# Squares of the norms summed over channel blocks on VectorE ahead of the ones-matmuls

## The reference

```python
D_MODEL = 1024
D_FF = 2816
EPS = 1e-6

def rmsnorm(x, g):
    xf = x.astype(jnp.float32)
    y = xf * lax.rsqrt(jnp.mean(xf * xf, axis=-1, keepdims=True) + EPS)
    return (y * g.astype(jnp.float32)).astype(x.dtype)

def swiglu(x, w_gate, w_up, w_down):
    return (jax.nn.silu(x @ w_gate) * (x @ w_up)) @ w_down

def trunk(h, pos, pool_prev, ret_prev, chunked):
    for i in range(DEPTH):
        xn = rmsnorm(h, norm_mix[i])
        if i % N_MIXERS == 0:
            mix, buf = multiscale_pool_mix(xn, ...)
        else:
            mix, s = retention_mix(xn, pos, ...)
        h = h + mix
        h = h + swiglu(rmsnorm(h, norm_ffn[i]), w_ffn_gate[i], w_ffn_up[i], w_ffn_down[i])
    return rmsnorm(h, norm_final), ...
```

## Time and profile before

| | |
|---|---|
| time, median of 3 runs | 1643.95 us (1643.01, 1643.95, 1694.63) |
| span of the profiled execution, slowest core (core 4) | 1656.3 us |
| spans of its 8 cores | 1629.7 to 1656.3 us |
| medians of the two dies | 1634.0 and 1640.6 us |
| PE busy on core 4 | 1594.7 us (96%) |
| DVE, ACT, POOL busy on core 4 | 735.8 (44%), 669.6 (40%), 355.5 us (21%) |
| mean granted TensorE clock, over the cores | 0.978 to 0.990 |

### The profile page before, as it was taken

One profiled execution on the slowest core, in us unless ns is written; L12 is line 12 of the kernel. 1 busy time (PEld: TensorE's weight loads), 2 busy tenths in 40 slices (PEclk: granted clock), 3 DMA queues, 4 the chain that ended last, 5 costly groups with the idle time before them and its releaser, 6 DMA issues.

```text
span 1656.3 us, 28455 instructions; the slowest of 8 cores (1629.7 to 1656.3 us)
## 1 busy us (share of the span) xinstructions
PE 1594.7 (96%) x9951; PEld 919.8 (56%) x10044; DVE 735.8 (44%) x1415; ACT 669.6 (40%) x1223; POOL 355.5 (21%) x584
## 2 busy tenths in 40 slices
PE   5999999999999989989999999999998899999997
PEld 3666666655555655444454444456554456666665
DVE  4432222634637362444363543356564556323225
ACT  4311022256465733545645424444664464110222
POOL 5110100334435221110101010013524146101000
PEclk8899999999999999999999999999999899999998
DMA  9157975787666778878989997876537531313432
GB/s 236 28 102 161 190 150 113 139 143 139 141 131 119 140 172 277 271 218 206 249 210 273 259 278 258 239 200 138 109 82 77 76 65 51 104 60 97 71 53 104
DMA packets 87449, 253.78 MB, mean 153 GB/s; under 512 B 17584, under 2 KB 24048, under 8 KB 87296
## 3 DMA queue, kind: packets, MB, share of 16 engines
q0 software_dynamic: 32656, 114.57, 37.2%
q1 hardware_dynamic: 54656, 137.40, 27.6%
HBM read 254.81 MB, written 73.27 MB: 198 GB/s over the span
## 4 chain that ended last, share of the span: by engine, by line
PE 89%; DMA 5%; DVE 2%; issue 2%; ACT 1%; POOL 1%; SPq 0%; DVEq 0%; POOLq 0%; ACTq 0%
PE pm L483 75%; PE psU L483 7%; PE psS L483 5%; DMA U<-U 2%; PE pm L491 1%; DMA cs_sb<-sret 1%; DMA cs_sb<-xtok 1%; DMA fb<-sret 1%; PE pm L487 0%; DMA fb<-xtok 0%; ACT on L500 0%; SPq L202 0%; DVE stt L982 0%; DVE hB L507 0%; DVE fb L516 0%
## 5 line engine op out<-in xcount | busy, mean ns | idle before, releaser
L483 PE MATMUL pm<-xn,w 128*128 128x512 bf16 (+8 forms) x4395 | 790.3, 337 | 3.7 <-DVE xn L516 1.1
L483 PEld LDWEIGHTS pm<-xn,w 128*128 128x128 bf16 x4432 | 433.5, 99 | 329.8 <-issue 20.8
L483 PE MATMUL pm<-U,w 128*128 128x512 bf16 (+6 forms) x2295 | 404.2, 333 | 4.0 <-DVE U L507 2.6
L483 PEld LDWEIGHTS pm<-U,w 128*128 128x128 bf16 x2310 | 224.2, 98 | 165.9 <-issue 21.7
L507 DVE TENSOR_TENSOR U<-pm,rot 128x512 bf16<-128x512 f32 (+5 forms) x206 | 121.2, 588 | 372.1 <-PE pm L483 344.0
L500 ACT ACTIVATE rot<-pm 128x512 bf16<-128x512 f32 (+6 forms) x190 | 98.3, 518 | 368.9 <-PE pm L483 364.5
L507 DVE TENSOR_TENSOR hB<-pm,hB 128x347 f32<-128x347 f32 (+4 forms) x143 | 76.2, 544 | 101.9 <-PE pm L483 101.1
L483 PE MATMUL pm<-w,xn 128*128 128x512 bf16 (+1 forms) x444 | 105.1, 381 | 1.1 <-DVE U L507 0.3
L507 POOL TENSOR_TENSOR U<-rot 128x352 bf16<-128x352 f32 (+2 forms) x96 | 93.1, 990 | 56.9 <-DVE rot L507 56.8
L507 DVE TENSOR_TENSOR hA<-pm,hA 128x512 f32<-128x512 f32 (+4 forms) x117 | 67.8, 588 | 83.3 <-PE pm L483 82.9
L507 DVE TENSOR_TENSOR rot<-pm,cs_sb 128x352 f32<-128x352 f32 (+2 forms) x170 | 79.3, 512 | 26.5 <-POOL U L507 14.8
(11 more groups left out here) (252 smaller groups left out, 1536.4 us busy)
## 6 DMA issues: line engine op xcount, KB each, us to landing
w<-c_gu POOLq DMA_DIRECT2D x49, 512.0 KB, 7.5
w<-w_gu POOLq DMA_DIRECT2D x39, 512.0 KB, 8.9
fb<-sret SPq DMA_DIRECT2D x38, 512.0 KB, 9.1
nrs<-fb SPq DMA_DIRECT2D x38, 512.0 KB, 9.3
w<-w_d POOLq DMA_DIRECT2D x32, 352.0 KB, 5.6
w<-c_d POOLq DMA_DIRECT2D x32, 352.0 KB, 6.1
c_gu<-w SPq DMA_DIRECT2D x17, 512.0 KB, 8.1
w<-w_qk POOLq DMA_DIRECT2D x16, 512.0 KB, 10.8
```

The lines of the kernel that those rows point to most:

```text
L483: return P.op('pe', lambda h: h.matmul(out, lhsT=lhsT, rhs=rhs, start=start, stop=stop, skip_group_check=skip), ins=[lhsT, rhs], outs=[out ...
```

## The change

`presum` adds squares of channel blocks to one another on DVE, in place and in bf16, as soon as `hadd` and the square of block m are recorded: at m = 2 block 1 += 0, at 3 block 2 += 1, at 4 block 3 += 2, at 6 block 5 += 4, at 7 block 6 += 5. Block 3 then holds the sum of blocks 0 to 3, block 6 that of 4 to 6, and block 7 is left as it is; `norm_stat` runs over blocks 3, 6 and 7. The norm after the pooling of `hA` keeps its eight. The sums over channels are rounded to bf16 at each addition.

```diff
--- before.py
+++ after.py
@@ -683,22 +683,30 @@
                     if e in handoff:
                         handoff.remove(e)
 
-        def norm_stat(r, sq, c0, n):
+        PRE = {2: (1, 0), 3: (2, 1), 4: (3, 2), 6: (5, 4), 7: (6, 5)}
+
+        def presum(sq, m, c0, n):
+
+            if m in PRE:
+                a, b = (sq[:, i, c0:c0 + n] for i in PRE[m])
+                tt(a, a, b, ALU.add)
+
+        def norm_stat(r, sq, c0, n, parts=(3, 6, 7)):
             pb = bank()
             tl = [(o, min(128, n - o)) for o in range(0, n, 128)]
             for i, (o, w) in enumerate(tl):
-                for c in range(8):
-                    mm(pb[0:w, i:i + 1], sq[:, c, c0 + o:c0 + o + w], onesb[:, 0:1], c == 0, c == 7)
+                for c in parts:
+                    mm(pb[0:w, i:i + 1], sq[:, c, c0 + o:c0 + o + w], onesb[:, 0:1], c == parts[0], c == parts[-1])
             return rsq(r[:, 0:len(tl)], pb[:, 0:len(tl)], 1024.0 * EPS, 128, len(tl))
 
-        def norm_gen(h, sq, wcol, c0, n, after=None, final=None, stat=None, pause=None):
+        def norm_gen(h, sq, wcol, c0, n, after=None, final=None, stat=None, pause=None, parts=(3, 6, 7)):
 
             yield after
             r = stat
             if r is None:
                 r = rs4[nrm['i'] % len(rs4)]
                 nrm['i'] += 1
-                yield norm_stat(r, sq, c0, n)
+                yield norm_stat(r, sq, c0, n, parts)
             if pause is not None:
                 yield 10 * pause
             tl = [(o, min(128, n - o)) for o in range(0, n, 128)]
@@ -830,7 +838,7 @@
                 late = [stat_a(i) for i in ahead[g:g + 1]]
                 if g < len(pumps):
                     wpump(pumps[g])
-            ng = norm_gen(hA, xn, C_NF0, c0, nt)
+            ng = norm_gen(hA, xn, C_NF0, c0, nt, parts=tuple(range(8)))
             yield next(ng)
             x = next(ng)
             for f in late:
@@ -939,6 +947,7 @@
                 hadd(h, m, c0, n, pb)
                 if last:
                     square(h, sq, m, c0, n)
+                    presum(sq, m, c0, n)
                 sd.poll()
             for fh in range(2):
                 j = 0
@@ -1219,6 +1228,7 @@
                 hadd(hh, m, c0, n, pb)
                 if exit_fn is not None:
                     sqlast[0] = tt(xn[:, m, c0:c0 + n], hh[:, m, c0:c0 + n], hh[:, m, c0:c0 + n], ALU.mult, "pool") if hf else square(hh, xn, m, c0, n)
+                    presum(xn, m, c0, n)
                 sd.poll()
             if exit_fn is not None:
                 for bi, (c0, n) in enumerate(blocks):
@@ -1460,6 +1470,7 @@
             for i, (c0, n) in enumerate(F512):
                 for m in range(8):
                     x = act(SQB[:, m, c0:c0 + n], hB[:, m, c0:c0 + n], ACT.Square)
+                    presum(SQB, m, c0, n)
                     yield 1.0
                 yield x
                 yield norm_stat(rsB[:, i, :], SQB, c0, n)
```

## The result

The changed kernel takes 1668.37 us (median of four runs, 1667.05 to 1675.89); the kernel before takes 1643.95 us (median of 1643.01, 1643.95 and 1646.16). Some runs of any of these kernels are slower, with a lower clock on the cores of a die (one run of before took 1694.63 us), and medians and ratios here are of the others. The ratio is 1.0148, 95% interval 1.012 to 1.0176: 1.5% slower, 24 us, where I had forecast 1638 us and a range of 1628 to 1649.

A forecast was written before the change was run, and what follows sets the result against it. PE was taken to bound the kernel, busy 1594.7 of 1656.3 us. From 1643.95 us, -9.1 for matmuls and +3.1 for the tail, additions hidden and reordering at nothing, gave 1638 us; range 1628 to 1649.

The forecast's parts named there:

- The removed matmuls: In the norm statistics on PE: 310 one-column matmuls fewer at 31 ns, 9.6 us, of which 9.1 us on the path.
- The first rival: DMA-heavy stages, 720 to 1130 us: saved matmuls only lengthen waits, losing up to 4.0 us; 1642 to 1647, chance 0.18.
- The added instructions: On DVE: 96 additions at 0.4 us, 38 us (20 to 54), hidden at nearly every stage end, priced at nothing.
- The third rival: Retention's last projection on `hB`: additions wait for POOL, up to 16 us, 1654; slower once over 6 reach PE; chance 0.09.
- The tail: Program's end, T being the last `hadd`'s end: six multiplies delay `rs_2`; last multiply from T + 7.7 to T + 10.8, 3.1 us longer.
- The second rival: Lower-clock stretches at 600 and 740 us, 3.4 us each: one gone 1635, both 1631, one more 1641; under 1633, chance 0.13.

The follow-up runs named there:

- mm_only: Kernel before in its old order, with three statistic matmuls for eight and no additions, so outputs change; 1637.48 us, ratio 0.9946 to before.
- adds_only: Kernel before in its old order, with all 96 additions and all eight matmuls kept, so outputs change; 1653.05 us, ratio 1.0044 to before.
- same_order: The whole change, with the planner's clocks kept so that the order is that of the kernel before; 1649.5 us, ratio 1.0034 to before.
- order_only: Instructions of the kernel before (eight matmuls, no additions) in the order the changed kernel's planner gives; 1665.94 us, ratio 1.0121 to before.
- exact_cost: The changed kernel with the planner told that a one-column matmul takes 0.031 us rather than 0.056; 1659.7 us, ratio 1.0095 to before.
- ffn_only: Old order; additions and three matmuls behind the FFNs and in the pooled half's statistic, but the old code behind the retentions; 1644.2 us, ratio 1.0014 to before.
- ffn_exits: Old order; additions and three matmuls only in norms behind the FFNs, not behind retentions or in the pooled half's statistic; 1645.68 us, ratio 1.001 to before.

## Why the prediction was wrong

**The removed matmuls: right.** 9.1 us were forecast; `mm_only` is 0.9946 of before, which is 8.9 us, and one costs 31 ns in both kernels. Where the Trainium skill, "TensorE: Matmul & The Clock Gate", section "Wait — 56ns, not 53.3ns?", has some 62 ns for matmuls that software decodes, the gain would be an estimated 19 us; the run excludes it. The first rival, the gain covered by transfers, is not borne out by the same run, whose gain is the whole 9 us; its interval, 5 to 13 us, leaves room for that rival's 4 us, and the stretches in question vary too much between cores to place them.

**The added instructions: the size too high, the cover too generous.** An addition at 341 to 347 columns takes 333 ns (0.40 forecast; DVE has 28 us more, 38 forecast). But they are not hidden everywhere: +7 us in `adds_only`, where the places behind the two retentions, in which DVE carries gates and statistics, take 3.2 and 3.3 us more, and PE waits 6.1 us a core for additions at the pooled half's statistic. I had looked at each stage end by itself and found room behind the last square, and had not asked what is queued around the addition in a retention and beside the state's products.

**The third rival: its mechanism is there, at a third of its price.** I gave additions that wait 1.1 us each for POOL up to 16 us. Measured are 4.8 us of waiting and additions stretched to 0.57 to 0.62 us, of which 3.3 us reach PE (88.5 to 91.8), about 1 of them POOL's doing. That stays below the rival's own turning point of 6. It is not what made the kernel slower. In the changed order 6.1 us are lost in that stretch, and on core 0 one wait of 4.4 us for a gate shows how; the chain is in DVE's timeline of after:

```profile
1388.56 0.81 DVE L507 TENSOR_TENSOR xn<-xn 128x347 bf16<-128x347 bf16 x1 [0.59 <-POOL xn L507]
1389.30 1.05 DVE L516 SCALAR_TENSOR_TENSOR xn<-hB,w,pm 128x347 bf16<-128x347 f32 x2
1390.27 0.51 DVE L507 TENSOR_TENSOR hB<-pm,hB 128x347 f32<-128x347 f32 x1
1390.70 0.32 DVE L507 TENSOR_TENSOR xn<-xn 128x347 bf16<-128x347 bf16 x1
1390.95 0.68 DVE L507 TENSOR_TENSOR U<-af,U 128x512 bf16<-128x512 f32 x1
```

```profile
1391.77 0.75 PE L483 MATMUL pm<-U,w 128*128 128x346 bf16 x4 [4.40 <-DVE U L507]
```

**The tail: right, and a little short.** Forecast was T + 10.8 for the last multiply's end and 3.1 us more. T is 1653.32 on core 4 of after, and the timeline has

```profile
1656.40 0.16 DVE L511 TENSOR_SCALAR rs<-pm 128x3 f32<-128x3 f32 x1
...
1658.61 4.95 DVE L516 SCALAR_TENSOR_TENSOR hB<-hB,w,pm 128x346 f32<-128x346 f32 x10 [1.08 <-PE pm L491]
```

`rs` at T + 3.1 (3.55 forecast) and the last multiply's end at 1663.56, T + 10.2, 2.5 us more than the T + 7.7 of before. The table's medians, which go on to the end of the last stores, give +3.7. `same_order` has 10.9: the tail's loss is all order.

**The step that failed** is this one: "In most places the rows are permuted by an instruction or two, and PE has other matmuls in between; I price that at nothing, with an uncertainty of some 4 us either way (a few waits of the size in the earlier trace rows, whose longest is 7.2 us)." I had even named a DMA transpose or state load issued later as what would make the prediction wrong, but bounded it by PE's waits and did not look through SyncE's list, where the transposes and their two neighbours stood in a new order. Costed by what the runs show: 10 us for the transposes, 4 for the two units of state, 2 for the norm's multiplies ahead of the first projection, 3 to 4.5 in the last part, 3 for the tail: 22 to 24 us, where `order_only` as a whole shows 20. The range's upper bound had room for half of the third rival (8 us) and some 3 us more, so it could not hold this. (Its closing sums are loose besides: twice the third rival is 1670 us, not 1677, and that rival's full price, 1654, lay outside the range.) The second step that failed is smaller: the additions were priced at nothing on the path, and cost 7. Why the units slipped is argued, not tried by itself: the planner charges 128 / 2400 + 0.003 = 0.056 us for a matmul that takes 0.031, so its clock lost 310 x 0.056 = 17 us where the chip's lost 10, and it charges the additions to DVE; two units fewer then fit in ahead of the retention. `exact_cost` shows that the charge of the matmuls alone isn't all of it.

**The clock.** The second rival expected slices at the lower level to vanish, and named one more as its other side (1641 us). It came the other way: in the first part of the retention of `hB` before is at full clock on all cores, and after spends 10 to 20 us of it at the lower level on each. Part of that falls into PE's waits; the work done in the rest lost an estimated 3 to 4 us.

What stays open is the layer 1 SwiGLU of `hA`, where medians of 256 to 273 us and a spread of 10 us and more between cores in most kernels hide effects of a few us; the intervals of `ffn_only` (0.9974 to 1.0054) and `ffn_exits` (0.9985 to 1.0036) leave open whether additions behind the SwiGLUs alone would gain or lose. Nor is it settled what makes the 4.5 us of the last part in the changed order without additions; on core 0, with 2.9 of them, 1.4 are one wait of PE for a gate.

## What to carry to other kernels

Where a planner or scheduler sets the order, a change of a few instructions is also a change of order, and the second can be worth twice the first: make one kernel that keeps the old order and one that has only the new, before reading anything into the sum. Compare the lists of the DMA queues first, row by row around every transfer that PE needs soon; a transfer issued 12 us ahead of its use, which slips by 9 us and so in among loads of half a megabyte, is dearer than hundreds of small matmuls, since it is not only issued later but takes 10 us instead of 3. And an addition "on an idle engine" is free only where nothing that PE awaits stands behind it in that engine's queue.

## What the hardware showed that I had not expected

- Moving two DMA transposes 8.7 us later, behind one load in their own queue and four in POOL's, took their time to landing from 2.8 to 9.6 us and cost 10.3 us on the whole, more than the 7.1 us wait that shows: the granted clock of the stretch fell from 1.00 to 0.96. In the changed kernel the clock falls 5 us into a wait of 8.5 and is back 2.8 us after it, so that of some 6 us at the lower level only the last 2.8 cost anything.
- Given precedence, the transposes were in time, and a state load was 2.4 to 12.9 us late instead; 8 of the 18 us came back. The DMA share is 1.12 and 1.01 in the two 10 us slices of the changed kernel above, and the order of the queue chose which transfer was late.
- The bf16 addition of two SBUF tiles of 347 columns takes 0.33 us, less than two thirds of an f32 addition from PSUM of the same width (0.52). Where POOL makes the squares, eight of 15 take 0.82 us and seven the same 0.33.
